# Shared stage of a routed-expert block: VectorE sums and adds a tile before it scales the older one, and ScalarE issues the row loads ahead of the square

## The reference, cut to what matters

```
x = x + merged @ w_o                                  # mixers, done long before
h2 = rmsnorm(x, g_ffn)
shared = (silu(h2 @ s_gate) * (h2 @ s_up)) @ s_down   # every token, hidden width 256
routed = routed_experts(h2, ...)                      # 8 of 64 experts for each token
x = x + (shared + routed)
y = rmsnorm(x, g_final)                               # x * rsqrt(mean(x*x) + EPS) * g_final
```

## Time and profile before

| what | value |
|---|---|
| median of 3 runs | 2720.7 us (2719.16 to 2722.24) |
| profiled execution | 2719.18 us |
| its span | 2717.5 us |
| around the span | 1.68 us |
| TensorE busy | 2622.4 us, 97% |
| VectorE busy | 1792.5 us, 66% |
| ScalarE busy | 1226.6 us, 45% |
| GpSimd busy | 1320.5 us, 49% |

### The profile page before, as it was taken

How to read it: one execution, slowest core, us unless ns; L and a number is a source line. 1 busy time by engine, 2 the same in 40 slices (tenths; PEclk the granted TensorE clock), 3 DMA queues, 4 the chain that set the end, 5 groups by cost and what they waited for, 6 DMA issues and landing times.

```text
span 2717.5 us, 51117 instructions
## 1 busy us (share of the span) xinstructions
PE 2622.4 (97%) x11902; PEld 2163.8 (80%) x11903; DVE 1792.5 (66%) x2537; ACT 1226.6 (45%) x1740; POOL 1320.5 (49%) x1093
## 2 busy tenths in 40 slices
PE   7999999999999999939999999999999999999997
PEld 6888888888888888727888888888888888888876
DVE  4544555655555655557877877777877777777577
ACT  3223323332323232215666666566665556666422
POOL 3000003110222013267877887777877777778622
PEclk9999999999999999959999999999999999999999
DMA  8223423442344224337988988888988888888675
GB/s 313 96 97 105 146 100 102 127 152 93 100 132 154 93 101 132 125 112 241 277 252 253 298 271 243 236 243 248 291 273 248 249 237 238 237 237 252 183 230 190
DMA packets 170046, 523.52 MB, mean 193 GB/s; under 512 B 37722, under 2 KB 43532, under 8 KB 170000
## 3 DMA queue, kind: packets, MB, share of 16 engines
q1 hardware_dynamic: 96208, 345.46, 35.0%
q0 software_dynamic: 65584, 163.32, 25.5%
q10 hardware_dynamic: 8208, 14.16, 1.6%
HBM read 434.94 MB, written 119.18 MB: 204 GB/s over the span
## 4 chain that ended last, share of the span: by engine, by line
PE 49%; DVE 3%; issue 1%; DMA 1%; POOL 1%; DVEq 1%; ACTq 1%; ACT 0%; POOLq 0%; SPq 0%
PE ps_gu L1502 11%; PE ps_gu L1500 11%; PE ps_gu L1501 11%; PE ps_y L1502 5%; PE ps_y L1501 5%; PE ps_y L1500 5%; PE ps_h L1556 1%; DVE xt L1714 1%; DVE xl L1725 1%; ACTq L1679 1%; POOL xs L1429 0%; DVEq L1788 0%; DMA xs<-h_dram,gidx 0%; DVE y L1790 0%; DVE y L1783 0%
## 5 line engine op out<-in xcount | busy, mean ns | idle before, releaser
L1429 POOL DMA_INDIRECT xs<-h_dram,gidx x656 | 828.0, 1262 | 202.0 <-issue 199.0
L1500 PE MATMUL ps_gu<-expert_hi,xl 128*128 (+1 forms) x1392 | 543.6, 391 | 22.2 <-DVE xl L1725 17.5
L1709 DVE TENSOR_TENSOR expert_lo<-expert_raw,expert_hi 128x1024 f32 (+1 forms) x390 | 459.7, 1221 | 133.4 <-ACT expert_hi L1586 128.9
L1502 PE MATMUL ps_gu<-expert_hi,xh 128*128 (+1 forms) x1392 | 543.5, 390 | 0.0
L1501 PE MATMUL ps_gu<-expert_lo,xh 128*128 (+1 forms) x1392 | 543.1, 390 | 0.0
L927 DVE TENSOR_TENSOR ul<-raw,uh 128x1024 fp32r<-128x1024 f32 x186 | 227.9, 1225 | 406.9 <-ACT uh L751 402.8
L1586 ACT ACTIVATE expert_hi<-expert_raw 128x1024 f32 (+1 forms) x390 | 391.2, 1053 | 78.2 <-PEq L1560 39.1
L95 POOL TENSOR_SCALAR rstd<-mean 128x1 f32<-128x1 f32 x29 | 6.6, 226 | 848.8 <-ACT junk L770 848.5
L514 PE MATMUL ps_t<-hh,ul 128*128 128x512 f32 x1024 | 401.9, 392 | 3.1 <-DVE wgl L1156 3.1
L515 PE MATMUL ps_t<-hl,uh 128*128 128x512 f32 x1024 | 399.4, 390 | 0.0
L516 PE MATMUL ps_t<-hh,uh 128*128 128x512 f32 x1024 | 399.3, 390 | 0.0
(11 more groups left out here) (272 smaller groups left out, 3941.4 us busy)
## 6 DMA issues: line engine op xcount, KB each, us to landing
expert_raw<-experts SPq DMA_DIRECT2D x396, 512.0 KB, 6.2
raw<-units SPq DMA_DIRECT2D x192, 512.0 KB
xs<-h_dram,gidx POOLq DMA_INDIRECT x656
h_dram<-h ACTq DMA_DIRECT2D x17, 512.0 KB, 4.4
acc_odd<-h POOLq DMA_DIRECT2D x17, 512.0 KB, 16.0
acc<-x SPq DMA_DIRECT2D x4, 2048.0 KB, 8.3
expert_raw<-acc_odd SPq DMA_DIRECT2D x16, 512.0 KB, 6.5
expert_raw<-x POOLq DMA_DIRECT2D x14, 512.0 KB, 3.7
```

Of the source, the lines that this page charges most:

```text
L1429: nc.gpsimd.indirect_dma_start(xs[s][:, g * DQ:(g + 1) * DQ], None, h2_quarters, bass.IndirectOffsetOnAxis(ap=gidx[s][:, g:g + 1], axis=0) ...
L1500: nc.tensor.matmul(out_, sl, vh, start=first, stop=False)
L1502: return nc.tensor.matmul(out_, sh, vh, start=False, stop=last)
L1709: V.tensor_tensor(l_, raw[:, p, :], h_, ALU.subtract).then_inc(piece_ready, 1)
```

## The change

Two moves within the written order, on two engines. No instruction is added or taken away, and no wait is.

```diff
@@ scalar, for t in range(2, NT) @@
                 if t == NT - 1:
                     hidden_high(n * 2 + t, t % 2)
-                square(t - 2)
                 if t + AHEAD - 1 < NT:
                     load_rows(t + AHEAD - 1)
+                square(t - 2)
@@ vector, for t in range(1, NT) @@
-                if 3 <= t <= LATE:
-                    scale(t - 3)
                 if t > LATE:
                     sum_tile(t - 1)
                 if 2 <= t <= LATE:
                     sum_tile(t - 2)
                 if t >= 2:
                     add_shared(t - 2)
+                if 3 <= t <= LATE:
+                    scale(t - 3)
                 if t == LATE:
                     sum_tile(t - 1)
```

## The result

The changed kernel took 2701.79 us (2700.55 to 2702.59, four runs) against 2720.22 us before: a ratio of 0.9935, 95% interval 0.9923 to 0.9946. A second set, taken later, gave 2703.76 against 2719.73 us, 0.9940 (0.9927 to 0.9954). I had expected 16.3 us; the two sets show 18.4 and 16.0. The profiled execution took 2701.0 us, its span is 2699.3 us.

What follows compares the result with a forecast made beforehand. A VectorE-ScalarE loop of 9.92 us bounds the shared stage; at 7.75 us it yields to TensorE's 8.41. Pace 10.75, stall 4.0, clock 1.6, less 0.1, make 16.3 us: 2720.7 − 16.3 = 2704.4 us, range 2701 to 2710.

Steps and rivals of the forecast that it cites:

- The row loads: ScalarE, shared stage: moved ahead of the square, their issues leave the loop, saving 1.01 us in each of nine steps.
- My lower bound: Cost of the row loads' issues in their new place ahead of ScalarE's square: nothing.
- the upper bound of 4.1 us: Row loads' four issues at 1.02 us each, ending 1.4 us behind the point where the square could start.
- rival (a): ScalarE: row loads keep 1 us on the loop, steps 8.76 us apart; gain 12.2, time 2708.5 us; chance 9%.
- (d): ScalarE: an issue ahead of the square blocks and holds the whole loop; slower, 2729 us; chance 2%.
- The scale: VectorE: behind the addition it saves 1.16 us in eleven steps, hidden beside square and sigmoid with 0.5 us to spare.
- The pace: Shared stage: loop falls from 9.92 to 7.75 us, TensorE leads at 8.41 from step 6; 10.75 us gained.
- The stall of 3.9 us: TensorE's tail, behind down(13): the 3.92 us stand-still goes (4.0 us gained), and the slow clock with it (1.6 us).
- The tail: End of the shared stage: addition of tile 14 starts at about 2690.6 instead of 2706.87, without waiting for the last reload.
- The 8.8 us: Tail: time from scale end through store to landed reload, so the last sum's data land at 2686.3, wanted at 2689.0.
- rival (b): Tail keeps TensorE's stall because a reload or GpSimd holds VectorE at t = 13 or 14; 2709.9 us; chance 6%.
- Rival (c): Shared stage: another wait holds the sigmoid, loop stays near 9.9 us, about 2 us gained; 2719 us; chance 5%.

Runs made afterwards that it cites:

- the row loads alone: Kernel before with only the row loads moved ahead of the square; 2732.16 against 2739.82 us (0.9963), repeat 2708.20 against 2717.86 us (0.9966).
- tile 10's scale back: Changed kernel with tile 10's scale alone ahead of the sum again; 2718.13 against 2739.82 us (0.9929), repeat 2700.16 against 2717.86 us (0.9938).
- the first tail experiment: Changed kernel with tile 10's scale ahead of the sum again and tile 13's behind tile 15's half additions; 2702.56 against 2719.73 us (0.9936).
- the scale alone: Changed kernel with row loads behind the square again; 2730.12 against 2739.82 us (0.996), repeat 2709.18 against 2717.86 us (0.9965).
- the dummy of 1024: Changed kernel plus an unneeded 128x1024 VectorE addition between sum and addition in steps 3 to 13; one execution, 2712.37 us.

## Why the prediction was right

The forecast of 2704.4 us and its mechanism held up to the last sigmoid, step by step; one step of the tail did not.

- The row loads cost nothing in front of the square: 1.77 to 2.55 us of issue in the changed kernel's two traces, and the square waits for the addition in every step. My lower bound was right there; the upper bound of 4.1 us wasn't far-fetched either. In three other traces a group took 3.1 to 3.6 us (one in the repeat of the row loads alone, one in the repeat of tile 10's scale back, two in the first tail experiment), and the square came 0.1 to 1.4 us late for it, the most here:

```profile
2613.27 3.59 ACTq L1679 DMA_DIRECT2D xs<-h_dram  x4
2617.09 1.06 ACT L1660 ACTIVATE junk<-y 128x1024 bf16<-128x1024 f32 x1 [6.40 <-issue]
```

  This is the mechanism of rivals (a) and (d), issues that hold the square, in a single step: it took 9.05 us, beyond TensorE's 8.41 but below the 9.92 of before. Of the six traces with both edits and no dummy two show it, and that neither is the changed kernel's own is partly luck. TensorE, which asks for the result a whole `gate_up` later, didn't stall, and the way to the last sigmoid stayed 109.29 us.
- The scale is hidden beside square and sigmoid, with 0.44 us of idle time behind it (0.5 was worked out).
- The pace: 7.7 us for the loop (7.75 said), TensorE leading from step 6 on, 109.29 us from sigmoid 2 to 15 (13 × 8.41 = 109.33 said).
- The stall of 3.9 us and the slow matmuls behind it are gone, together.
- The tail was 1.1 us too short in my sum, 16.7 against 17.8 us behind the last sigmoid. The step that failed is "The reload for that last sum lands at 2677.5 + 8.8 = 2686.3 and is wanted at 2689.0: no wait". The 8.8 us came from rows in which the store landed in 3.2 us and the load in 4.5; they took 6.5 and 5.4, so that scale end to landed reload came to 13.0 us: 4.2 us more, with 2.7 us of room in the sum. With tile 10's scale back in its place the wait is gone and the tail is 16.8 us, as the sum had it. This is a small piece of rival (b)'s mechanism, without the stall.
- The experiment with the scale alone has the pace that rival (a) gave, steps of 8.7 to 9.0 us, but with the row loads still behind the square; rival (a) itself, a price in the new place, shows only in the single steps above. Rival (c) is excluded by the sigmoids that wait for TensorE.

That the first set moved by 18.4 and not by 16.3 us goes, by the two profiled executions, to 3.0 us ahead of the stage; the other runs have no trace. The changed kernel's two traces have sigmoid 2 at 2572.2 and 2575.6 us, the first of the kernel before at 2575.2. So how near the time came to 2704.4 us is partly luck: this spread is larger than the 1.1 us that the sum was off. The stage, 15.2 us in both traces of the changed kernel against the first of before, is the fair test of it (16.4 us against the second, whose clock stayed low for longer in the tail).

## What to carry to other kernels

When two engines pass work round a loop, find the loop by the instruction whose releaser is "issue" or the other engine though its real data are long there, and move what isn't needed on it into the idle time that the list of waits shows: the gain is the smaller of the sum of the moved pieces and the distance to the next bound. When work is moved behind something, follow each buffer that it frees to the store and the reload behind it, with a landing time measured while other transfers run, not alone. On an in-order engine, what is moved late holds everything written behind it, on the engine that waits for it too.

## What the runs showed of the hardware

The same stall of 3.9 us has had different prices. After it, the clock stayed at the 1.2 GHz level for nine matmuls in the first trace of the kernel before, and for thirteen in the second, of which these are the transposes, the first matmul, the thirteenth, and the next:

```profile
2710.75 0.66 PE L1556 MATMUL ps_h<-eye,hid 128*128 128x128 f32 x2 [3.91 <-DVE htl L1740]
2711.06 0.78 PE L1500 MATMUL ps_y<-expert_hi,htl 128*128 128x512 f32 x1
...
2716.32 0.53 PE L1500 MATMUL ps_y<-expert_hi,htl 128*128 128x512 f32 x1
2716.69 0.39 PE L1501 MATMUL ps_y<-expert_lo,hth 128*128 128x512 f32 x1
```

The granted clock was 0.50 from 2711.06 to 2716.32 us. That is 1.0 us more behind the last sigmoid, 20.02 against 18.98 us. Behind the same stall of 3.9 us thirteen matmuls were slow in the repeat of the row loads alone, and seven each in its first trace and with the dummy of 1024. The stall in the experiment with the scale alone was followed by slow matmuls when it was 2.97 us (first trace), and by none when it was 2.00 us (repeat). Groups of four DMA issues that read the same amount took from 1.77 to 3.59 us on ScalarE, and a store of 512 KB landed in 2.9 to 3.2 us with its neighbours about 3 us or more away, and in 6.5 us with a load issued 0.2 us ahead of it.
